# Groups of four, later sums and half-size GpSimd subtractions around the norms of a two-layer diffusion backbone step

## The chip, the cores and the metric

The kernel runs on one core of a Trainium2 chip, in one launch. The metric is the device time in microseconds; executions of one kernel are compared by their median.

## The reference, cut to what matters

The kernel computes one inference step for 512 latent and 128 context tokens of width 1024, in float32. Layer 0 has a Conformer convolution and a bidirectional retention behind one input projection; layer 1 has grouped-query attention with per-head RMS norms and rotary positions. Each layer ends in an MLP of width 4096, and a norm stands before every projection:

```python
for layer in range(DEPTH):
    sh1, sc1, g1, sh2, sc2, g2 = ...
    h = rmsnorm(x, norm_g[layer, 0]) * (1 + sc1) + sh1
    y = even_mixer(h, ...) if layer % 2 == 0 else blocked_attention(*gqa_project(h, ...)) @ odd_w_o[li]
    x = x + g1 * y
    h = rmsnorm(x, norm_g[layer, 1]) * (1 + sc2) + sh2
    x = x + g2 * (jnp.square(jax.nn.relu(h @ mlp_w1[layer])) @ mlp_w2[layer])
return rmsnorm(x, final_g), new_ret, new_k, new_v
```

## The kernel before

**Layout and precision.** The trunk x lies transposed in SBUF as xT, 8 chunks of 128 features by 640 tokens, and is worked on in two halves of 320 tokens. Each product keeps float32 accuracy by splitting both factors into a high and a low part (hH, hL; wH, wL) and adding three matmuls for each chunk k: high by high, high by low, low by high (product, L471). A group is one PSUM bank's result: 8 chunks, 24 matmuls. acc_full counts finished groups.

**Weights.** 96 tiles of 1024 x 256 pass through two slots (t % 2). For each, SyncE loads two halves into raw (load_tile, L350), ScalarE copies a half to wH (split, L977), and GpSimd subtracts to make wL (lo, L1361, L1366), one instruction of 1024 columns for each half, counted by wl_done. A split may begin only when the groups that read its slot are done; on ScalarE it stands in a fixed place among the evictions, with an acc_full value to wait for.

**A norm.** There are four with a projection behind them: norm 0 (the gate's projection), 1 (MLP of layer 0), 2 (QKV), 3 (MLP of layer 1). While the tile before still runs, VectorE adds its products to xT (residual, L1382), ScalarE squares xT (square, L985), VectorE adds the squares to ssum (add_squares, L1392), TensorE multiplies ssum by ones (stat, L598), ScalarE takes the root (std, L994), VectorE the reciprocal (L1409). Then for each half and chunk: VectorE makes vb (h_value, L1419), ScalarE hH (hi, L999), VectorE hL (h_lo, L1429), which counts h_ready. VectorE's order, with the residuals and squares of the second half put between the chunks of the first, is written out by hand in h_both (L1442), called from pair_ends (L1695) and for norm 1 at L1715. ScalarE's is in before_pair_ends (L1008), for norm 1 at L1163, and behind the norm in mlp_layer (L1223), the gate's lines (L1044) and the QKV loop (L1281).

**Behind a norm** TensorE does two weight tiles as a pair, so that the first half of h is used four times before the second is needed: tile_pair (L520) has groups 0 to 3 on half 0 (tile 0, tile 0, tile 1, tile 1) and 4 to 7 on half 1, two groups interleaved by k. stat(norm, 1) for the second half stands inside the first two groups, ahead of k = 4. The first half of the groups waits for banks by dve_free, the second by act_free. Slot 0 is released with group 5 and slot 1 with group 7: split(t0 + 2, 0, g0 + 6) and split(t0 + 3, 1, g0 + 8). In the MLP, ScalarE evicts a group with a relu to fr (L1219, two buffers), VectorE squares it to fs (L1735), ScalarE copies to fH (L1213), VectorE subtracts to fL (L1728). For the gate the eviction is a sigmoid (gate_out, L1049).

**QKV** (qkv_pair, L559) has the tokens in rows and 256 columns: ten groups, (tile, token block), in the order of QKV_PAIR, of which tile 0 makes the keys. Four more tiles follow (tile_n, L545; L897). VectorE norms and rotates each result (rope, L1782; its root is rope_std on ScalarE, L1255), TensorE turns it (turn_keys, L871, inside the first of the four tiles; turn_queries, L883, behind each), and ScalarE copies it out (turned_out, L1259, counted by tr_out, for which the next turn waits).

**Retention and convolution** (L1530 to L1624) run beside twelve weight tiles; VectorE does the convolution's 31 taps (L1543) there, 124 instructions of 655 columns.

## Time and profile before

| | |
|---|---|
| time of three runs | 1694.05 us median (1691.47 to 1695.34) |
| the profiled execution: its own time | 1695.47 us |
| its span | 1693.7 us |
| granted TensorE clock, mean over the span | 0.98 |
| TensorE busy | 1619.5 us (96%) |
| VectorE, ScalarE, GpSimd busy | 770.2, 528.1, 503.2 us |
| share of TensorE in the chain that ended last | 86% |

A row of a timeline gives start and duration in microseconds, engine, line, operation, output and inputs; equal neighbours are merged (x2), and the brackets give the idle time before it and what ended it. PE is TensorE, DVE VectorE, ACT ScalarE, POOL GpSimd. PEclk is the granted clock of TensorE as a share of its full 2.4 GHz.

### The profile page before, as it was taken

To read this page: it belongs to the slowest core of one execution; us is meant where nothing else is said; L and a number is where in the kernel's file an instruction comes from. 1 tells how busy PE (TensorE), PEld (TensorE's weight loads), DVE (VectorE), ACT (ScalarE), POOL (GpSimd) and SP (SyncE) were. 2 spreads that over 40 slices of the span, in tenths; PEclk is the share of its full clock that TensorE was granted. 3 is DMA by queue.
4 is the path that set the end of the run, shared out by engine and by line. 5 is a ranking of instruction groups with operands and counts; after the bars stand their busy time and mean duration, and the time that the engine had idled before them with its cause. 6 is when DMAs were issued, how large, how long until landed. Compare 5 with 4: busy or idle time off the path is not lost.

```text
span 1693.7 us, 27621 instructions
## 1 busy us (share of the span) xinstructions
PE 1619.5 (96%) x11934; PEld 1539.0 (91%) x11934; DVE 770.2 (45%) x1438; ACT 528.1 (31%) x986; POOL 503.2 (30%) x198
## 2 busy tenths in 40 slices
PE   5899998989899999999999989999999999999998
PEld 3899998979899999999999889556999999999997
DVE  4547675656662232242232865653572241331333
ACT  3413332324442132131232423543352131231332
POOL 0335234313233333333323233000233333333331
PEclk8999999999999999999999999999999999999999
DMA  8444333202243233343343122000222222222221
GB/s 298 141 158 127 117 113 125 88 26 69 87 149 125 94 132 125 125 148 105 105 142 111 57 75 69 13 1 1 79 85 75 75 76 75 75 75 75 75 75 63
DMA packets 131019, 162.16 MB, mean 96 GB/s; under 512 B 4433, under 2 KB 103633, under 8 KB 130897
## 3 DMA queue, kind: packets, MB, share of 16 engines
q1 hardware_dynamic: 129664, 159.34, 29.0%
q8 instruction: 94, 1.54, 0.4%
q10 hardware_dynamic: 1232, 1.05, 0.2%
q14 instruction: 29, 0.23, 0.0%
HBM read 156.44 MB, written 3.93 MB: 95 GB/s over the span
## 4 chain that ended last, share of the span: by engine, by line
PE 86%; DVE 8%; ACT 2%; POOL 1%; DMA 1%; issue 1%; SPq 0%; DVEq 0%; ACTq 0%
PE ps L479 74%; PE ps L590 2%; PE ps L944 2%; DVE hL L1429 2%; POOL wL L1366 1%; PE ps L909 1%; DMA pre_over_h<-in_ada_w 1%; PE ps L685 1%; DVE amx L1819 1%; PE ps L718 1%; DVE vb L1419 1%; ACT wH L983 1%; PE ps L610 1%; PE ps L923 1%; DVE xT L1387 1%
## 5 line engine op out<-in xcount | busy, mean ns | idle before, releaser
L1366 POOL TENSOR_TENSOR wL<-raw,wH 128x1024 fp32r<-128x1024 f32 x192 | 500.2, 2626 | 1158.1 <-ACT wH L983 1157.9
L479 PE MATMUL ps<-hH,wH 128*128 128x320 f32 x1536 | 482.6, 314 | 12.5 <-DVE hL L1429 7.1
L479 PE MATMUL ps<-hL,wH 128*128 128x320 f32 x1536 | 477.3, 311 | 0.0
L479 PE MATMUL ps<-hH,wL 128*128 128x320 f32 x1536 | 477.3, 311 | 0.0
L479 PE MATMUL ps<-fH,wH 128*128 128x320 f32 x1024 | 317.6, 310 | 0.0
L479 PE MATMUL ps<-fH,wL 128*128 128x320 f32 x1024 | 316.2, 309 | 0.0
L479 PE MATMUL ps<-fL,wH 128*128 128x320 f32 x1024 | 316.2, 309 | 0.0
L479 PEld LDWEIGHTS ps<-hH,wH 128*128 128x128 f32 x1536 | 291.2, 190 | 19.4 <-issue 9.5
L983 ACT ACTIVATE wH<-raw 128x1024 fp32r<-128x1024 f32 x192 | 193.0, 1051 | 346.9 <-PE ps L479 328.9
L479 PEld LDWEIGHTS ps<-hL,wH 128*128 128x128 f32 x1536 | 291.1, 190 | 0.6 <-issue 0.4
L479 PEld LDWEIGHTS ps<-hH,wL 128*128 128x128 f32 x1536 | 290.8, 189 | 0.0
L1387 DVE SCALAR_TENSOR_TENSOR xT<-ps,modT,xT 128x320 f32<-128x320 f32 (+2 forms) x264 | 107.4, 436 | 388.3 <-PE ps L479 388.2
L1735 DVE TENSOR_TENSOR fs<-fr 128x320 f32<-128x320 f32 x128 | 79.4, 621 | 265.0 <-ACT fr L1219 264.1
L479 PEld LDWEIGHTS ps<-fH,wH 128*128 128x128 f32 x1024 | 192.5, 188 | 1.7 <-issue 1.6
L479 PEld LDWEIGHTS ps<-fL,wH 128*128 128x128 f32 x1024 | 192.5, 188 | 0.1
L479 PEld LDWEIGHTS ps<-fH,wL 128*128 128x128 f32 x1024 | 192.5, 188 | 0.0
L479 PE MATMUL ps<-wH,hH 128*128 128x256 f32 x560 | 164.6, 294 | 4.8 <-POOL wL L1366 4.3
L479 PE MATMUL ps<-wL,hH 128*128 128x256 f32 x560 | 160.2, 286 | 0.0
L479 PE MATMUL ps<-wH,hL 128*128 128x256 f32 x560 | 160.2, 286 | 0.0
L1219 ACT ACTIVATE fr<-ps 128x320 f32<-128x320 f32 x128 | 55.7, 437 | 279.3 <-PE ps L479 279.2
L479 PEld LDWEIGHTS ps<-wH,hH 128*128 128x128 f32 x560 | 109.4, 195 | 6.4 <-issue 4.0
L479 PEld LDWEIGHTS ps<-wL,hH 128*128 128x128 f32 x560 | 109.4, 195 | 0.5 <-issue 0.2
(190 smaller groups left out, 1591.5 us busy)
## 6 DMA issues: line engine op xcount, KB each, us to landing
raw<-in_mlp_w SPq DMA_DIRECT2D x128, 512.0 KB, 3.9
ada<-in_ada_w SPq DMA_DIRECT2D x40, 1024.0 KB, 5.2
raw<-in_even_w_in SPq DMA_DIRECT2D x32, 512.0 KB, 5.8
raw<-in_even_w_out SPq DMA_DIRECT2D x12, 512.0 KB, 3.6
raw<-in_odd_w_qkv SPq DMA_DIRECT2D x12, 512.0 KB, 3.6
pre_over_h<-in_ada_w SPq DMA_DIRECT2D x2, 2048.0 KB, 14.9
pre_arena<-in_ada_w SPq DMA_DIRECT2D x2, 2048.0 KB, 18.7
raw<-in_odd_w_o SPq DMA_DIRECT2D x8, 512.0 KB, 3.4
```

The costliest lines, as they stand in the source:

```text
L479: last = nc.tensor.matmul(ps[:, bank, 0:width], a_, b_, start=(k == 0 and p_ == 0), stop=(k == nk - 1 and p_ == 2))
L590: last = nc.tensor.matmul(ps[32 * j:32 * j + 32, B_ADA, 0:P], siluc[:, 4 * part + k, :], by_lane[:, j], start=(part == 0 and k == 0), stop ...
L610: return nc.tensor.transpose(ps[:, bank, at:at + np_], src[p0:p0 + np_, tile, col0:col0 + P], ident[p0:p0 + np_, p0:p0 + np_])
L685: return nc.tensor.matmul(ps[:, bank, at:at + RV], kd_nat[:, r, tile, :], v_nat[:, tile, :], start=True, stop=True)
L718: last = nc.tensor.matmul(out, qdec[:, r, cs], S[:, r, n, :], start=False, stop=(r == 1))
L944: last = nc.tensor.matmul(ps[:, 6, :], va[:, vt, kv * P:(kv + 1) * P], pT[:, h % 2, n, :], start=(n == 0), stop=(n == 4))
L983: nc.scalar.activation(wH[:, slot, j * 1024:(j + 1) * 1024], raw[:, j, :], ACT.Copy).then_inc(wh_done, 1)
L1219: nc.scalar.activation(fr[:, n % 2, :], ps[:, n % 4, 0:HALF], ACT.Relu).then_inc(act_free, 1)
L1366: nc.gpsimd.tensor_tensor(wL[:, slot, cs], raw[:, j, :], wH[:, slot, cs].bitcast(F32), ALU.subtract).then_inc(wl_done, 1)
L1387: last = nc.vector.scalar_tensor_tensor(out=x, in0=ps[:, n % 4, c0 - half * HALF:c0 - half * HALF + w_], scalar=modT[:, gate_at + k, which ...
L1429: last = nc.vector.scalar_tensor_tensor(out=hL[:, k, c0:c0 + w_], in0=vb[:, k % 4, a_:a_ + w_], scalar=modT[:, SHIFT_AT[norm] + k, which:w ...
L1735: nc.vector.tensor_tensor(fs[:, n % 2, :], fr[:, n % 2, :], fr[:, n % 2, :], ALU.mult).then_inc(fs_done, 1)
```

## The change

- In all four pairs, the groups of the second half (4 to 7) are interleaved by k as one group of four, waiting for each bank at k = 0 (product's free). QKV_PAIR is reordered so that its groups 4 to 7 are token blocks 2 and 3 of both tiles, and 8 and 9 block 4.
- stat(norm, 1) stands ahead of k = 6 instead of k = 4, for norms 1, 2 and 3.
- ScalarE evicts groups 2 and 3 between the chunks of hH of the second half, fr has four buffers, and the splits of the next two tiles stand behind group 7's eviction (behind groups 8 and 9 for QKV).
- The orders of squares, hH chunks and splits before norms 1 to 3, and VectorE's order of residuals, squares and chunks, are changed.
- GpSimd subtracts in two pieces of 512 for each half tile.
- The first rotation waits for group 8 (act_free + 9) instead of 6, the keys are turned behind tile T_QKV + 2, and turn_queries(0) stands behind group 1 of the tile after, with turned_out(0) behind that group's eviction.

```diff
--- before.py
+++ after.py
@@ -104,7 +104,7 @@
 NAT_BANKS = (0, 1, 2, 3, 7)
-QKV_PAIR = ((0, 0), (0, 1), (1, 0), (1, 1), (0, 2), (0, 3), (0, 4), (1, 2), (1, 3), (1, 4))
+QKV_PAIR = ((0, 0), (0, 1), (1, 0), (1, 1), (0, 2), (0, 3), (1, 2), (1, 3), (0, 4), (1, 4))
@@ -249,7 +249,7 @@
         fL = place("fL", [P, KC, T], F32R)
-        fr = place("fr", [P, 2, HALF])
+        fr = place("fr", [P, 4, HALF])
@@ -468,12 +468,14 @@
         def _(pe):
-            def product(groups, nk, waits, width):
+            def product(groups, nk, waits, width, free=None):
...
                     waits(k)
-                    for bank, lhs, rhs in groups:
+                    for n, (bank, lhs, rhs) in enumerate(groups):
+                        if free and k == 0:
+                            free[n]()
@@ -517,7 +519,7 @@
-            def tile_pair(t, xH, xL, free, x_wait=None, hooks=None, nk=KC, nm=2, inside=None, together=1):
+            def tile_pair(t, xH, xL, free, x_wait=None, hooks=None, nk=KC, nm=2, inside=None, joint=None):
@@ -526,9 +528,11 @@
-                for n in range(0, 4 * nm, together):
-                    for q in range(n, n + together):
-                        free(q)
+                for ns in joint or [(n,) for n in range(4 * nm)]:
+                    n = ns[0]
+                    if len(ns) < 4:
+                        for q in ns:
+                            free(q)
@@ -537,8 +541,8 @@
                             x_wait(n // (2 * nm), n // nm % 2, k)
-                    product([group(q) for q in range(n, n + together)], nk, waits, HALF)
-                    for q in range(n, n + together):
+                    product([group(q) for q in ns], nk, waits, HALF, [lambda q=q: free(q) for q in ns] if len(ns) == 4 else None)
+                    for q in ns:
@@ -565,9 +569,10 @@
-                for ns in ((0, 1), (2, 3), (4, 5), (6,), (7, 8), (9,)):
-                    for q in ns:
-                        free(q)
+                for ns in ((0, 1), (2, 3), (4, 5, 6, 7), (8, 9)):
+                    if len(ns) < 4:
+                        for q in ns:
+                            free(q)
@@ -576,7 +581,7 @@
                             x_wait(n // 4, k)
-                    product([group(q) for q in ns], KC, waits, 256)
+                    product([group(q) for q in ns], KC, waits, 256, [lambda q=q: free(q) for q in ns] if len(ns) == 4 else None)
@@ -661,7 +666,7 @@
                       lambda half, tile, k: pe.wait_ge(h_ready, 8 * half + k + 1),
-                      {1: [lambda: strips(0)], 5: [lambda: strips(1)]}, together=2)
+                      {1: [lambda: strips(0)], 3: [lambda: strips(1)]}, joint=((0, 1), (2, 3), (4, 5, 6, 7)))
@@ -852,7 +857,7 @@
                           {1: [lambda: strips(M_MLP)], 3: [lambda: strips(M_MLP + 1)]} if layer == 0 else None,
-                          inside=(0, 4, lambda: stat(norm, 1, SUMS)), together=2)
+                          inside=(0, 6, lambda: stat(norm, 1, SUMS)), joint=((0, 1), (2, 3), (4, 5, 6, 7)))
@@ -893,11 +898,14 @@
                      pe.wait_ge(act_free, A_QKV + n - 4) if n > 4 else None,
-                     lambda half, k: pe.wait_ge(h_ready, 16 * 2 + 8 * half + k + 1), (0, 4, lambda: stat(2, 1, SUMS)))
+                     lambda half, k: pe.wait_ge(h_ready, 16 * 2 + 8 * half + k + 1), (0, 6, lambda: stat(2, 1, SUMS)))
...
                 tile_n(T_QKV + t, t % 2, lambda n, t=t: pe.wait_ge(act_free, A_QKV + 5 * (t - 1) + n + 1), NAT_BANKS,
-                       {1: [turn_keys]} if t == 2 else None)
-                turn_queries(t - 2)
+                       {1: [lambda: turn_queries(0)]} if t == 3 else None)
+                if t == 2:
+                    turn_keys()
+                else:
+                    turn_queries(t - 2)
@@ -1008,15 +1016,18 @@
                 std(norm, 0)
-                hi(norm, 0, range(0, 3))
                 square(norm, 12, v0, "tile")
+                hi(norm, 0, (0,))
                 square(norm, 13, v0, "tile")
+                hi(norm, 0, (1,))
                 split(t, 0, start - 2)
-                hi(norm, 0, range(3, 6))
+                hi(norm, 0, (2, 3))
                 square(norm, 14, v0, "tile")
+                hi(norm, 0, (4,))
+                split(t + 1, 1, start)
+                hi(norm, 0, (5,))
                 square(norm, 15, v0, "tile")
-                split(t + 1, 1, start)
-                hi(norm, 0, range(6, 8))
+                hi(norm, 0, (6, 7))
@@ -1044,7 +1055,6 @@
             hi(0, 0, range(6, 8))
-            hi(0, 1, range(0, 4))
@@ -1054,13 +1064,14 @@
             gate_out(1)
-            hi(0, 1, range(4, 8))
-            for n in range(2, 6):
+            hi(0, 1, range(0, 3))
+            gate_out(2)
+            gate_out(3)
+            hi(0, 1, range(3, 8))
+            for n in range(4, 8):
                 gate_out(n)
-            split(2, 0, G_GATE + 6)
-            gate_out(6)
-            gate_out(7)
-            split(3, 1, G_GATE + 8)
+            split(2, 0)
+            split(3, 1)
@@ -1165,18 +1176,20 @@
             square(1, 9, V_WC, "half")
-            hi(1, 0, range(0, 2))
+            hi(1, 0, (0, 1))
             square(1, 10, V_WC, "half")
-            hi(1, 0, range(2, 4))
             square(1, 11, V_WC, "half")
+            hi(1, 0, (2,))
             split(T_MLP0, 0, G_WC + 12)
+            hi(1, 0, (3,))
             square(1, 12, V_WC, "half")
-            hi(1, 0, range(4, 6))
+            hi(1, 0, (4,))
             square(1, 13, V_WC, "half")
+            split(T_MLP0 + 1, 1, G_MLP0)
+            hi(1, 0, (5,))
...
             square(1, 15, V_WC, "half")
-            split(T_MLP0 + 1, 1, G_MLP0)
-            hi(1, 0, range(6, 8))
+            hi(1, 0, (6, 7))
@@ -1214,23 +1227,24 @@
                     act.wait_ge(acc_full, g0 + 32 * g + n + 1)
-                    if n >= 2:
-                        act.wait_ge(fs_done, f0 + 16 * g + n - 1)
-                    nc.scalar.activation(fr[:, n % 2, :], ps[:, n % 4, 0:HALF], ACT.Relu).then_inc(act_free, 1)
-                    if n > 1 or g and n:
+                    if n >= 4:
+                        act.wait_ge(fs_done, f0 + 16 * g + n - 3)
+                    nc.scalar.activation(fr[:, n % 4, :], ps[:, n % 4, 0:HALF], ACT.Relu).then_inc(act_free, 1)
+                    if n and (g or n > 3):
...
-                hi(norm, 1, range(0, 4))
...
                 relu(0, 1)
-                hi(norm, 1, range(4, 8))
-                hidden_hi(0, 0)
-                for n in range(2, 6):
+                hi(norm, 1, range(0, 3))
+                relu(0, 2)
+                relu(0, 3)
+                hi(norm, 1, range(3, 8))
+                for n in range(3):
+                    hidden_hi(0, n)
+                for n in range(4, 8):
                     relu(0, n)
-                split(t0 + 2, 0, g0 + 6)
-                relu(0, 6)
-                relu(0, 7)
-                split(t0 + 3, 1, g0 + 8)
+                split(t0 + 2, 0)
+                split(t0 + 3, 1)
@@ -1278,24 +1292,25 @@
-            hi(2, 1, range(0, 2))
...
                 qkv_out(n, *QKV_PAIR[n], NAT_BANKS[QKV_BANK[n]])
-                if n == 0:
-                    hi(2, 1, range(2, 4))
                 if n == 1:
-                    hi(2, 1, range(4, 8))
-                if n == 6:
-                    split(T_QKV + 2, 0, G_QKV + 7)
+                    hi(2, 1, range(0, 2))
+                if n == 3:
+                    hi(2, 1, range(2, 8))
+                if n == 8:
+                    split(T_QKV + 2, 0, G_QKV + 9)
+            split(T_QKV + 3, 1, G_QKV + 10)
             rope_std(0)
-            split(T_QKV + 3, 1, G_QKV + 10)
...
                         rope_std(t - 1)
-                    if n == (3 if t == 2 else 1):
-                        turned_out(t - 2)
+                    if n == 1 and t > 2:
+                        turned_out(t - 3 if t == 3 else t - 2)
+                    if n == 3 and t == 3:
+                        turned_out(1)
@@ -1362,9 +1377,11 @@
                     pool.wait_ge(wh_done, 2 * t + j + 1)
-                    cs = slice(j * 1024, (j + 1) * 1024)
-                    nc.gpsimd.tensor_tensor(wL[:, slot, cs], raw[:, j, :], wH[:, slot, cs].bitcast(F32),
-                                            ALU.subtract).then_inc(wl_done, 1)
+                    for c0 in (0, 512):
+                        cs = slice(j * 1024 + c0, j * 1024 + c0 + 512)
+                        last = nc.gpsimd.tensor_tensor(wL[:, slot, cs], raw[:, j, c0:c0 + 512], wH[:, slot, cs].bitcast(F32),
+                                                       ALU.subtract)
+                    last.then_inc(wl_done, 1)
@@ -1441,6 +1458,8 @@
+                for step in later.get("first", ()):
+                    step()
@@ -1702,8 +1721,8 @@
-                h_both(norm, {0: [lambda: update(first + 4)], 2: [lambda: update(first + 5)], 3: [squares(2)],
-                              5: [lambda: update(first + 6)], 6: [lambda: update(first + 7)], 7: [squares(3)]})
+                h_both(norm, {0: [lambda: update(first + 4)], 1: [lambda: update(first + 5)], 3: [squares(2)],
+                              4: [lambda: update(first + 6)], 6: [lambda: update(first + 7)], 7: [squares(3)]})
@@ -1712,10 +1731,12 @@
                     add_squares(1, n // 2, "half")
-            h_both(1, {0: [lambda: wc(8)], 1: [lambda: wc(9), lambda: add_squares(1, 4, "half")],
-                       3: [lambda: wc(10)], 4: [lambda: wc(11), lambda: add_squares(1, 5, "half")],
-                       5: [lambda: wc(12)], 6: [lambda: wc(13), lambda: add_squares(1, 6, "half"), lambda: wc(14)],
-                       7: [lambda: wc(15), lambda: add_squares(1, 7, "half")]})
+            def wc_squares(q):
+                return lambda: add_squares(1, q, "half")
+
+            h_both(1, {"first": [lambda: wc(8)], 0: [lambda: wc(9), lambda: wc(10)], 1: [lambda: wc(11)],
+                       2: [wc_squares(4), lambda: wc(12)], 3: [lambda: wc(13), wc_squares(5)], 4: [lambda: wc(14)],
+                       5: [lambda: wc(15)], 6: [wc_squares(6)], 7: [wc_squares(7)]})
@@ -1732,7 +1753,7 @@
                             dve.wait_ge(f_ready, f0 + 16 * g + n - 1)
-                        nc.vector.tensor_tensor(fs[:, n % 2, :], fr[:, n % 2, :], fr[:, n % 2, :], ALU.mult).then_inc(fs_done, 1)
+                        nc.vector.tensor_tensor(fs[:, n % 2, :], fr[:, n % 4, :], fr[:, n % 4, :], ALU.mult).then_inc(fs_done, 1)
@@ -1784,7 +1805,7 @@
                 tab = tabs[:, 1 if r == 0 else 0]
-                dve.wait_ge(act_free, A_QKV + (5 * r + 5 if r else 7))
+                dve.wait_ge(act_free, A_QKV + (5 * r + 5 if r else 9))
...

```

## Rows read from the trace of the kernel before

**Rows 1.** The page, part 1: busy time, share of span, instructions of each engine.
```profile
PE 1619.5 (96%) x11934; PEld 1539.0 (91%) x11934; DVE 770.2 (45%) x1438; ACT 528.1 (31%) x986; POOL 503.2 (30%) x198
```

**Rows 2.** The list of waits: engine, line, releaser: us in total, times, longest.
```profile
PE ps L601 <- DVE ssum L1405: 9.9, 3, 4.0
...
PE ps L479 <- DVE hL L1429: 7.6, 6, 4.1
...
PE ps L479 <- DVE xT L1387: 5.4, 1, 5.4
...
PE ps L877 <- DVE kro L1808: 5.5, 1, 5.5
...
PE ps L479 <- POOL wL L1366: 4.3, 2, 3.6
...
PE ps L913 <- ACT qTa L1270: 2.5, 1, 2.5
```

**Rows 3.** Windows: length, busy us (count) of PE, PEld, DVE, ACT, POOL, PEclk, DMA.
```profile
1223.60:1236.20 12.60, 9.41 (x51) 8.39 (x50) 11.96 (x16) 5.32 (x9) 7.29 (x3) 0.86 0.43 129
...
944.70:957.40 12.70, 9.32 (x53) 8.44 (x52) 12.08 (x16) 5.29 (x9) 7.27 (x3) 0.73 0.48 147
...
460.10:471.70 11.60, 10.30 (x54) 9.69 (x58) 9.68 (x14) 4.57 (x8) 4.99 (x2) 0.79 0.16 46
...
263.70:270.50 6.80, 6.11 (x51) 5.24 (x50) 0.00 (x0) 2.39 (x3) 4.27 (x3) 0.50 0.50 150
...
992.30:997.50 5.20, 5.19 (x25) 5.20 (x26) 4.73 (x5) 0.30 (x1) 0.00 (x0) 0.50 0.02 3
```

**Rows 4.** TensorE timeline, last norm, two starts 24 matmuls apart: start, us, instruction.
```profile
1248.11 0.31 PE L479 MATMUL ps<-hH,wH 128*128 128x320 f32 x1
...
1251.63 0.31 PE L479 MATMUL ps<-hH,wH 128*128 128x320 f32 x1
```

**Rows 5.** VectorE timeline, last norm; and the group of full-width hL (busy, mean ns).
```profile
1228.54 0.54 DVE L1429 SCALAR_TENSOR_TENSOR hL<-vb,modT,hH 128x320 fp32r<-128x320 f32 x1
...
1231.08 4.12 DVE L1429 SCALAR_TENSOR_TENSOR hL<-vb,modT,hH 128x320 fp32r<-128x320 f32 x2 [0.61 <-ACT hH L1004]
...
L1429 DVE SCALAR_TENSOR_TENSOR hL<-vb,modT,hH 128x320 fp32r<-128x320 f32 x32 | 39.3, 1238 | 4.8 <-ACT hH L1004 4.8
```

**Rows 6.** GpSimd timeline, a plain tile and one beside the taps; its 128x512 group.
```profile
1253.01 4.79 POOL L1366 TENSOR_TENSOR wL<-raw,wH 128x1024 fp32r<-128x1024 f32 x2 [18.16 <-ACT wH L983]
...
244.82 19.68 POOL L1366 TENSOR_TENSOR wL<-raw,wH 128x1024 fp32r<-128x1024 f32 x2 [8.76 <-ACT wH L983]
...
L1374 POOL TENSOR_TENSOR y_nat<-y_nat,gfin 128x512 f32<-128x512 f32 x2 | 2.7, 1392 | 16.6 <-ACT y_nat L1196 16.6
```

**Rows 7.** VectorE timeline, norm 1: the residual update that releases TensorE.
```profile
459.34 0.66 DVE L1387 SCALAR_TENSOR_TENSOR xT<-ps,modT,xT 128x192 f32<-128x192 f32 x2
```

**Rows 8.** ScalarE timeline, last norm, behind groups 4 and 5.
```profile
1250.51 0.47 ACT L1213 ACTIVATE fH<-fs 128x320 fp32r<-128x320 f32 x1
...
1250.88 0.42 ACT L1219 ACTIVATE fr<-ps 128x320 f32<-128x320 f32 x1
...
1251.88 2.00 ACT L983 ACTIVATE wH<-raw 128x1024 fp32r<-128x1024 f32 x2
```

**Rows 9.** ScalarE timeline, gate norm, behind group 5.
```profile
73.16 0.88 ACT L1052 ACTIVATE sgate<-ps 128x320 f32<-128x320 f32 x2 [2.62 <-PE ps L479]
```

**Rows 10.** VectorE and ScalarE timelines, keys' and queries' rotation.
```profile
972.97 1.49 DVE L1788 TENSOR_TENSOR rn<-k_nat 128x1280 f32<-128x1280 f32 x1 [1.23 <-ACT k_nat L1279]
...
983.50 2.91 DVE L1804 TENSOR_TENSOR kro<-rn,tabs 128x640 f32<-128x640 f32 x1
...
989.23 0.81 DVE L1804 TENSOR_TENSOR kro<-rn,tabs 128x640 f32<-128x640 f32 x1
...
1002.03 0.39 ACT L1279 ACTIVATE q_nat<-ps 128x256 f32<-128x256 f32 x1 [2.49 <-PE ps L479]
...
1002.31 1.08 ACT L1264 ACTIVATE kTa<-ps 128x512 f32<-128x512 f32 x2
```

## The prediction

> **What bounds the kernel now.** I read the page first: TensorE is busy 96% of the span [rows 1], so time comes only from its idle time and its half-rate stretches. The list of waits then names what it waits for [rows 2]: the lower half of h, the keys' rotation, the residual, ssum, weight tiles and qTa. Around the norms that the change touches lie most of these (the last one, for qTa, and the weight tile do not). The windows show their size. From the end of the tile before to the end of the first two groups, the last norm takes 12.6 us and the QKV norm 12.7 [rows 3]. A group is 24 matmuls; 24 starts lie 3.52 us apart [rows 4], 0.147 each, and at 256 columns instead of 320 I take 0.8 of that, 0.12. So 48 matmuls need 7.0 and 5.8 us, and 5.6 and 6.9 us are lost. At norm 1 the loss is the 5.4 us wait [rows 2] and 11.6 - 7.0 = 4.6 us more [rows 3]. Behind the 3.6 us wait for a weight tile the granted clock stood at 0.50, which is 1.2 GHz, for 6.8 us, and behind the one for kro for 5.2 us of running matmuls [rows 3]. Half rate costs half of that, 3.4 and 2.6 us; I take 2.7, since a fall that begins within the wait leaves less behind it.
>
> The VectorE timeline shows why h is late [rows 5]. An undisturbed hL takes 0.54 us; the two at 1231.08 take 4.12 together; TensorE's last k of the first groups needs the second of them. The mean over the 32 full-width ones is 1238 ns, so (1.24 - 0.54) x 32 / 4 = 5.6 us per norm are spent blocked. GpSimd's subtractions lie exactly there [rows 6].
>
> **Parts that gain.** (a) *Pieces of 512.* One subtraction of 1024 takes 2.40 us. A piece costs between half of that (1.20) and the 1392 ns of the one 128x512 GpSimd group [rows 6]; I take 1.25, since the shorter of that group's two is 1.29. A blocked hL then waits for 1.25 at most. Per norm I expect some four blocks of 0.5 to 0.6 left of the 6.6 us in norms 2 and 3: a gain of 4.4 us each (bounds 0 and 6.6). The Trainium skill ("SBUF — State Buffer", "Who interferes with whom") says that a VectorE instruction with two SBUF inputs and a GpSimd one that reads SBUF exclude each other for the whole instruction. By that rule the shorter piece caps each block; the trace agrees (0.54 against 2.06 us for hL).
>
> (b) *Sums later, VectorE order.* stat(norm, 1) moves from k = 4 to k = 6. Part of the 9.9 us that TensorE waits for ssum [rows 2] goes, but the k's behind it need hL anyway, and the last hL comes later than the last sum. Alone it is worth the clock fall at most; I count it within the 4.4. At norm 1 the update that TensorE waited for ended at 460.0 [rows 7], 5.4 us after the tile's end. It moves ahead by some 8 us; then the weight is the bound (two copies and 2.5 us of GpSimd behind square 11), near the tile's end, and after that hL, which I carry forward as 4.8 us earlier (bounds 0 and the whole 10.0).
>
> (c) Gate norm: the last hL of the first half is blocked likewise; one piece less gives 1.1.
>
> (d) *Keys later.* The 5.5 us wait for kro [rows 2] and the 2.6 of clock behind it [rows 3] go: 8.1.
>
> Gains: 1.1 + 4.8 + 4.4 + 4.4 + 8.1 = 22.8 us.
>
> **Parts that cost.** (e) *Groups of four.* Groups 4 to 7 use both weight slots until their last k. Before, slot 0 was free after group 5, two groups (7.0 us) before the pair's end, and its split ran beside groups 6 and 7. Now split(2, 0) and split(t0+2, 0) stand behind the last eviction, and TensorE has nothing else to do but wait for wL. From the start that TensorE's next matmul could have (0): the first eviction can begin at -1.1 (three times 3 matmuls earlier, less 0.2 to notice). At the MLP norms ScalarE does four relus at 0.43 and four fH copies at 0.47 [rows 8], which ends at 2.5, then half a split, 1.0, then two pieces, 2.5, and 0.2 of semaphores: 6.2. After 12 matmuls (8.0) the second half of the weights (8.7) holds it 0.7 more: 6.9 us each. At the gate it is four sigmoids at 0.44 [rows 9] in place of eight instructions: 0.7 + 1.0 + 2.5 + 0.2 = 4.4, and 0.7: 5.1. At QKV the pair (8, 9) ends the stage, and the split is behind group 8: 4.4 again for the first half; the second stands against rope(0)'s VectorE work, where VectorE's and GpSimd's instructions take turns (a product of 0.81 took 2.91 [rows 10]), so 2.1 more: 6.5. The quads' own gain, more time for each k of the second half, is at most a few tenths: the six waits for hL [rows 2] lie ahead of first halves or within them, but for one.
>
> (f) *Clock behind these.* The same kind of stall, 3.6 us for a weight tile [rows 2], was followed by 6.8 us at 0.50 [rows 3]. Four stalls at 2.7: 10.8 us (bounds 0 and 3.4 each).
>
> (g) *Queries.* turn_queries(0) now stands after group 1 of the next tile and needs turned_out(0), which ScalarE does only behind that group's eviction and behind rope_std(2). At least 0.39 for that eviction and 0.54 x 3 for the copies [rows 10], with 0.7 for the root and the semaphores 2.7 us, pass with TensorE idle. But rope_std(2) waits for VectorE's third rope, and the first one now starts some 8.6 us (three groups) later relative to TensorE, since the k_nat copies end with group 8. A rope is 1.49 x 3 + 0.81 x 6, about 10 us with its waits, more while pieces alternate with it (the 2.91 again). Carried forward, the wait is up to 9.6. I take 7.0, nearer the upper end because POOL is busy beside the first rope for six pieces, and 2.7 for the clock: 9.7.
>
> (h) In the convolution (130 to 340 us) a piece more has to get its turn: one stall of 3.6 us becomes 0.5 longer.
>
> Costs: 5.1 + 6.9 + 6.9 + 6.5 + 10.8 + 9.7 + 0.5 = 46.4. Net +23.6 us. The profiled execution took 1695.5 (span 1693.7 and 1.8 around it), so 1719.1; it lies 1.4 above the median of the runs shown, so 1717.7 against that median. Called 1718. What lies beside other work costs nothing: fr's two more buffers, SP's loads (raw is filled one tile ahead), and the doubled count of GpSimd instructions (0.1 more for two pieces, on an engine busy 30% [rows 1]).
>
> **Rivals.** *A milder loss:* the clock stays up behind most new stalls and turn_queries(0) waits for ScalarE alone. Then 23.6 - 10.8 - 2.7 - 4.3 = +6 with all clock falls gone, +9 with one left: about 1703. For it: the wait for turned_out alone is as short as the 2.5 us for qTa [rows 2]. Against: the weight stall of 3.6 us had its fall, and the new ones are longer.
>
> *Starved pieces:* GpSimd's two subtractions at 244.8 took 19.7 us together [rows 6], because VectorE's taps followed one another without a break. Where the first of two pieces gets in and the second does not, a weight tile comes late by a run of taps, up to the 15 us that were waited there (19.7 less 2 x 2.4). I put it at 9: 1727. Against: a piece gets in whenever VectorE waits for TensorE, as it does in this stage once for each head. The skill's rule in the same section, that whichever issues first gets the ports, knows no starvation and would leave this out; the 19.7 us speak against it here.
>
> *The other side, faster:* all loss before the first two groups' ends goes (5.6 + 6.9 + 10.0 + 1.1 + 8.1 = 31.7) and the clock stays up behind the new stalls, which are then 5.1 + 6.9 + 6.9 + 4.4 + 2.7 = 26.0: 5.7 us faster, 1688. The place is the wait for wL after each group of four; it decides when the sum of those stalls falls below the gain. Against: the first k's of a norm need hL within a microsecond of the reciprocal, and VectorE has 12 us of work [rows 3] in a stretch where TensorE needs 7.
>
> *The sums and pieces do not do what they say* (PE stays bound by the same last hL): gains 9.2 instead of 22.8, 1731.
>
> **Numbers.** Likeliest +24 (0.68; its own range 1706 to 1730), milder 0.12, starved 0.07, no gain at the norms 0.06, faster 0.07. The likeliest gives the time, 1718. Adding the milder case below and the two above gives 1700 to 1734; what lies outside, the faster case and the tails, is under 0.2. A measurement of this kernel tells a change of over 0.2% (3.4 us) from none. Faster by that 0.05; within it 0.04; slower 0.91.
>
> **What would show it.** After each norm's last group of four, a wait of TensorE for wL, 4 to 7 us, where rows 2 have 4.3 in all; half-rate stretches behind them; GpSimd 128x512 x384 with a mean near 1.3; the mean of hL from 1238 to below 900 ns; the wait for kro gone and one for kTa or qro at turn_queries(0). Wrong if TensorE goes on without a gap after those groups, or if that wait is under 3 us.

## The result, and the profile after

| | before | after |
|---|---|---|
| median of 4 runs, us | 1694.69 (1691.47 to 1695.43) | 1734.03 (1732.38 to 1736.44) |
| profiled execution's span, us | 1693.7 | 1734.6 |
| mean granted clock | 0.980 | 0.968 |

The ratio is 1.0235, 95% interval 1.0221 to 1.025: the change makes the kernel 39 us slower, where 24 were forecast. The time lies just above the upper end of the forecast's range, 1734.

First the page of the changed kernel, part 1, against [rows 1]:

```profile
PE 1630.6 (94%) x11934; PEld 1547.5 (89%) x11934; DVE 736.4 (42%) x1438; ACT 529.4 (31%) x986; POOL 544.4 (31%) x390
```

TensorE has the same 11934 matmuls and 94% of a longer span: idle time and half-rate time came on top. VectorE's busy time fell by 34 us: its instructions stand behind shorter GpSimd pieces, and the kernel before with these pieces alone, further below, has 731.4 us. Nothing came of it. The group of full-width hL has a mean of 793 ns where [rows 5] has 1238, and 15.2 us of idle time ahead where 4.8 stood:

```profile
L1446 DVE SCALAR_TENSOR_TENSOR hL<-vb,modT,hH 128x320 fp32r<-128x320 f32 x32 | 25.3, 793 | 15.2 <-ACT hH L1012 15.2
```

The list of TensorE's waits (columns as in [rows 2]) shows what was added:

```profile
PE ps L481 <- POOL wL L1382: 24.8, 6, 5.8
PE ps L481 <- DVE hL L1446: 19.3, 5, 5.3
PE ps L894 <- ACT kTa L1281: 11.1, 1, 11.1
...
PE ps L606 <- DVE ssum L1422: 4.3, 2, 3.9
PE ps L595 <- DMA ada<-in_ada_w: 4.2, 2, 3.6
```

Three are the forecast ones: wL from 4.3 to 24.8 us, kTa in place of kro, and ssum from 9.9 down to 4.3. Two are not: hL went up from 7.6 to 19.3 us, and the waits for a transfer of ada from 1.2 to 4.2 us. Where the time went can be read more closely by setting the n-th matmul of one trace against the n-th of the other. The lag is how much later a matmul starts in the changed kernel. It stands still between the stages, and each stage below is taken from one such level to the next:

| stage | forecast, us | grown lag, us |
|---|---|---|
| gate (norm 0 to its third tile) | +6.7 | +10.6 |
| norm 1 | -4.8 | -1.5 |
| behind MLP 0's group of four | +9.6 | +7.8 |
| norm 2 | -4.4 | +1.1 |
| behind QKV's group of four | +9.2 | +5.6 |
| keys | -8.1 | -8.0 |
| first queries | +9.7 | +12.5 |
| norm 3 | -4.4 | +3.4 |
| behind MLP 1's group of four | +9.6 | +7.6 |
| convolution | +0.5 | -1.6 |

The second column adds up to 37.5; 3.5 more lie scattered, 2.3 of them ahead of the gate, and the last matmul is 41.0 us late. Of the gate's 10.6, its norm is -1.0 and the rest +11.5. The three norms behind it brought a loss of 3.0 us where a gain of 13.6 was forecast. That difference of 16.6 us is as large as the whole error, 39 less 24.

Behind a group of four the forecast chain is there. At MLP 0 the last matmul starts at 505.06, ScalarE's split stands behind the last eviction, then come two pieces of GpSimd, then TensorE:

```profile
505.06 0.31 PE L481 MATMUL ps<-hH,wL 128*128 128x320 f32 x1
...
507.46 1.99 ACT L991 ACTIVATE wH<-raw 128x1024 fp32r<-128x1024 f32 x2
...
508.58 4.95 POOL L1382 TENSOR_TENSOR wL<-raw,wH 128x512 fp32r<-128x512 f32 x4 [31.61 <-ACT wH L991]
...
511.21 0.61 PE L481 MATMUL ps<-hH,wH 128*128 128x320 f32 x1 [5.83 <-POOL wL L1382]
511.61 0.47 PE L481 MATMUL ps<-hL,wH 128*128 128x320 f32 x1
511.88 0.47 PE L481 MATMUL ps<-hH,wL 128*128 128x320 f32 x1
```

What TensorE waits for at norm 3 is a lower half of h, behind the split that the change moved. ScalarE's timeline there (start, us, instruction, idle before and releaser):

```profile
1253.68 0.56 ACT L1012 ACTIVATE hH<-vb,modT 128x320 fp32r<-128x320 f32 x1
1256.15 1.06 ACT L991 ACTIVATE wH<-raw 128x1024 fp32r<-128x1024 f32 x1 [1.91 <-DMA raw<-in_mlp_w]
1260.58 1.06 ACT L991 ACTIVATE wH<-raw 128x1024 fp32r<-128x1024 f32 x1 [3.37 <-DMA raw<-in_mlp_w]
1261.55 0.55 ACT L1012 ACTIVATE hH<-vb,modT 128x320 fp32r<-128x320 f32 x1
```

and GpSimd's, VectorE's and TensorE's, a few rows each:

```profile
1249.42 5.85 POOL L1382 TENSOR_TENSOR wL<-raw,wH 128x512 fp32r<-128x512 f32 x4 [17.14 <-ACT wH L991]
1257.29 2.50 POOL L1382 TENSOR_TENSOR wL<-raw,wH 128x512 fp32r<-128x512 f32 x2 [2.02 <-ACT wH L991]
...
1262.12 1.21 DVE L1446 SCALAR_TENSOR_TENSOR hL<-vb,modT,hH 128x320 fp32r<-128x320 f32 x1 [5.46 <-ACT hH L1012]
...
1257.76 0.31 PE L481 MATMUL ps<-hH,wL 128*128 128x320 f32 x1
1263.39 0.64 PE L481 MATMUL ps<-hH,wH 128*128 128x320 f32 x1 [5.32 <-DVE hL L1446]
```

The split of the second tile now stands ahead of hi for k = 5. Its first cast waits 1.91 us and its second 3.37 us for raw to be filled: GpSimd had been reading raw for the tile before until 1255.27. ScalarE works in order, so hH for k = 5 comes at 1261.55, VectorE has been idle for 5.46 us, and TensorE for 5.32. Of all casts of MLP weights, the list of ScalarE's waits says, for before and for after (10.1 us of the latter at norms 1 and 3, and 13.9 behind the two groups of four):

```profile
ACT wH L983 <- DMA raw<-in_mlp_w: 3.5, 3, 1.5
```

```profile
ACT wH L991 <- DMA raw<-in_mlp_w: 24.0, 8, 5.5
```

At the gate, SP's own timeline shows the second thing that was missed, with TensorE's rows beside it:

```profile
87.86 2.84 SPq L356 DMA_DIRECT2D raw<-in_even_w_in  x2
90.75 8.47 SPq L368 DMA_DIRECT2D ada<-in_ada_w  x2
...
87.98 0.38 PE L481 MATMUL ps<-hH,wH 128*128 128x320 f32 x1 [4.13 <-POOL wL L1382]
...
96.86 1.94 PE L595 MATMUL ps<-ada,siluc 128*32 128x128 f32 x32 [3.59 <-DMA ada<-in_ada_w]
```

The fourth weight tile's load may be issued only when GpSimd has done with the third's raw, which the group of four made late; the ada load is the next thing in the same queue. So one late tile gives two waits. (The kernel before waits 1.2 us for the same transfer.) Windows (columns as in [rows 3]) at norm 1, behind MLP 0's group of four, at norm 3 and at the gate's second wait:

```profile
474.10:480.90 6.80, 4.97 (x15) 4.13 (x16) 5.63 (x7) 2.75 (x7) 2.75 (x2) 0.50 0.00 1
511.20:515.00 3.80, 3.79 (x14) 3.80 (x15) 0.00 (x0) 0.20 (x1) 2.33 (x2) 0.50 0.51 148
1262.50:1269.30 6.80, 5.87 (x19) 5.03 (x20) 6.15 (x7) 1.53 (x4) 1.97 (x2) 0.50 0.33 103
95.20:102.00 6.80, 5.14 (x44) 4.67 (x45) 0.00 (x0) 0.04 (x1) 2.56 (x3) 0.50 0.40 129
```

Each of these waits has a stretch at 1.2 GHz around it; the forecast expected such stretches only behind the groups of four and the queries.

### The profile page after: what moved, and what is told of

It is laid out like the page before. It is cut to its first block, busy times and chain, and to the rows that moved or that the text cites. A ratio compares the mean times of both kernels' runs of the same rounds, so it can differ in the third digit from the quotient of the medians.

```text
span 1734.6 us, 27787 instructions
## 1 busy us (share of the span) xinstructions
PE 1630.6 (94%) x11934; PEld 1547.5 (89%) x11934; DVE 736.4 (42%) x1438; ACT 529.4 (31%) x986; POOL 544.4 (31%) x390
## 4 chain that ended last, share of the span: by engine, by line
PE 85%; DVE 5%; POOL 3%; DMA 3%; ACT 2%; issue 1%; SPq 0%; DVEq 0%; ACTq 0%
PE ps L481 74%; POOL wL L1382 3%; PE ps L595 2%; PE ps L952 2%; PE ps L917 1%; DMA pre_over_h<-in_ada_w 1%; PE ps L690 1%; DVE amx L1840 1%; DMA ada<-in_ada_w 1%; PE ps L723 1%; ACT wH L991 1%; PE ps L615 1%; PE ps L931 1%; PE ps L651 1%; DMA raw<-in_mlp_w 1%
## 5 line engine op out<-in xcount | busy, mean ns | idle before, releaser
L1382 POOL TENSOR_TENSOR wL<-raw,wH 128x512 fp32r<-128x512 f32 x384 | 541.5, 1442 | 1158.1 <-ACT wH L991 1157.9
L1756 DVE TENSOR_TENSOR fs<-fr 128x320 f32<-128x320 f32 x128 | 74.2, 581 | 300.0 <-ACT fr L1232 298.9
L481 PEld LDWEIGHTS ps<-wH,hH 128*128 128x128 f32 x560 | 109.4, 195 | 14.6 <-issue 8.4
```

The source lines that it names most:

```text
L481: last = nc.tensor.matmul(ps[:, bank, 0:width], a_, b_, start=(k == 0 and p_ == 0), stop=(k == nk - 1 and p_ == 2))
L1382: last = nc.gpsimd.tensor_tensor(wL[:, slot, cs], raw[:, j, c0:c0 + 512], wH[:, slot, cs].bitcast(F32), ALU.subtract)
L1756: nc.vector.tensor_tensor(fs[:, n % 2, :], fr[:, n % 4, :], fr[:, n % 4, :], ALU.mult).then_inc(fs_done, 1)
```

## The experiments

Every kernel was timed against the kernel before on its chip, and a ratio to before is given with its 95% interval. A gain over the changed kernel is the difference of the two ratios times 1694 us (the changed kernel's is 1.0235); with both intervals it is good to some 4 us.

### The groups of four

Pairs everywhere, then at the gate alone, then at the two MLPs alone. In the changed kernel:

```diff
-joint=((0, 1), (2, 3), (4, 5, 6, 7)))
+joint=((0, 1), (2, 3), (4, 5), (6, 7)))
-                for n in range(4, 8):
-                    relu(0, n)
-                split(t0 + 2, 0)
-                split(t0 + 3, 1)
+                for n in range(2, 6):
+                    relu(0, n)
+                split(t0 + 2, 0, g0 + 6)
+                relu(0, 6)
+                relu(0, 7)
+                split(t0 + 3, 1, g0 + 8)
```

and likewise the evictions of the gate and QKV, with the order of hi halves around them. For QKV the first rope's root and the group for which the first rotation waits go back as well, so this run undoes a little more than the groups.

> The changed kernel with its second halves in pairs again: gate, both MLPs and QKV take (4, 5), (6, 7) where it has (4, 5, 6, 7), and the order of evictions, hi halves and splits around them goes back with it. The sums asked for later, the pieces of 512, the split ahead of hi 5 and the keys turned one tile later stay. Theory (the groups of four cost the waits for the weights of tile t+2 behind them, 4.1, 5.8, 4.3 and 5.8 us with their spells of half clock, the wait for ada at the gate's third tile, and the late third rope): gate 11 us, MLPs 6 and 7, QKV 5, queries 9 back, so 30 to 38 us faster than the changed kernel, 1696 to 1704 us. Rival (the waits for weights come from the pieces and GpSimd's later start, not from the groups): the waits for wL stay over 4 us each and the gain stays under 15 us, 1719 us or more. Rival two: pairs bring back the waits of the kernel before at the halves (7.6 us for hL in all) and the gain is 20 to 25 us.

Measured: 1699.92 us, 1.0039 (1.0024 to 1.0054), 33 us faster than the changed kernel, the size that the theory gave. The waits for wL fell from 24.8 us to this, with the convolution's old one in it:

```profile
PE ps L481 <- POOL wL L1382: 5.0, 3, 3.8
```

The wait at the first queries stayed, 8.5 us instead of 11.1, so most of it is not the groups' doing and that part of the theory fell; nor did the waits for hL go: 17.5 us.

> The changed kernel with its gate alone in pairs (4, 5), (6, 7) again, with the order of evictions, hi halves and splits of the kernel before there; MLPs and QKV keep their groups of four. Theory (by the two traces compared matmul by matmul the gate loses 11.8 us: 4.1 us for wL of the third tile, 3.7 for ada, the rest the two spells of half clock around them): 10 to 13 us faster than the changed kernel, 1721 to 1724 us, no wait for ada. Rival (the ada load ahead of the fourth weight tile gave 9.2 us by itself, so the group of four costs only what is left of it beside that load, or the two overlap less): 15 us or more faster, under 1719 us. Rival two (the gate's loss is only its two waits, 7.8 us): 7 to 9 us, 1725 to 1727 us.

Measured: 1724.10 us, 1.0168 (1.0145 to 1.0192): 11.3 us, the theory's, and the 11.5 of the lags. The wait for wL is gone, and the one for ada is 1.5 us, near the 1.2 of the kernel before, though SP's order is the changed kernel's.

> The changed kernel with the two MLPs alone in pairs again (evictions, hi halves and splits with them); gate and QKV keep their groups of four. Theory (the waits for wL of 5.8 us behind each group, with the half clock at both, 6.1 and 7.1 us by matmul): 11 to 15 us faster than the changed kernel, 1719 to 1723 us. Rival (the prediction's term, 6.9 us of wait and 2.7 us of clock each): 18 to 20 us, 1714 to 1716 us. Rival two (undone here, the wait for weights returns one tile on, since GpSimd is behind anyway): under 7 us, 1727 us or more.

Measured: 1718.40 us, 1.0137 (1.0116 to 1.0157): 16.6 us, between the theory (11 to 15) and the forecast's own term (18 to 20), and within 4 us of both. The lags give 7.8 + 7.6 = 15.4. What is left of the 33 us for QKV and the queries is 33.2 - 11.3 - 16.6 = 5.3, a rough figure since it is made of three such differences; QKV's group alone was not undone in any run.

### The place of the split at the norms

One place back, behind square 15. In the changed kernel, and likewise at norm 1:

```diff
                 hi(norm, 0, (4,))
-                split(t + 1, 1, start)
                 hi(norm, 0, (5,))
                 square(norm, 15, v0, "tile")
+                split(t + 1, 1, start)
                 hi(norm, 0, (6, 7))
```

> The changed kernel with one thing undone: at norms 1 to 3 the cast-and-copy pair of the second weight tile (split of tile t+1) stands behind square 15 again, not ahead of the fifth hi half. Theory (ScalarE, which works in order, stands ahead of hi 5 waiting for raw's transfer, 3.0 and 1.8 us at norm 1, 1.9 and 3.4 us at norm 3, so hH and hL of k = 5 come late): TensorE's waits for hL of 4.66, 4.77 and 5.32 us at the three norms fall to under 1.5 us each, the 0.5 clock behind them at two of the three goes: 10 to 13 us faster than the changed kernel, some 1721 to 1724 us. Rival (VectorE's own chain of halves sets the waits, and the split's place is nothing to it): the three waits stay over 4 us, the time within 2 us of 1734. Second rival: the split put back delays the weights of tile t+1 and the wait turns up at the next tile's first weights, the sum within 4 us of 1734.

Measured: 1730.13 us, 1.0215 (1.0195 to 1.0235): 3.4 us, no more. The theory asked for 10 to 13, so as it stood it fell. The waits for hL shrank only to 3.2, 3.4 and 2.6 us, and they had moved from k = 5 to k = 6. ScalarE's timeline at norm 1 shows what still stands ahead of hi 6:

```profile
469.60 1.04 ACT L991 ACTIVATE wH<-raw 128x1024 fp32r<-128x1024 f32 x1
471.75 1.06 ACT L991 ACTIVATE wH<-raw 128x1024 fp32r<-128x1024 f32 x1 [1.11 <-DMA raw<-in_mlp_w]
472.71 1.00 ACT L1012 ACTIVATE hH<-vb,modT 128x320 fp32r<-128x320 f32 x2
```

Two casts and one transfer, 3.1 us from the first cast's start to that of hi 6. So the next kernel puts the split behind hi 6 and 7 as well:

```diff
                 square(norm, 15, v0, "tile")
-                split(t + 1, 1, start)
                 hi(norm, 0, (6, 7))
+                split(t + 1, 1, start)
```

> The changed kernel with the split of the second weight tile at norms 1 to 3 behind all hi halves of the first half (k = 6 and 7 too); one place earlier, behind square 15, its two casts still stood ahead of hi 6 and one of them waited 1.1 us for raw's transfer, so that TensorE's wait only moved from k = 5 to k = 6 (3.2, 3.4 and 2.6 us) and 3.9 us came back. Theory (ScalarE in order behind a cast that needs raw is the whole of these waits): the three waits fall to under 1.2 us each, 8 to 12 us faster than the changed kernel, 1722 to 1726 us. Rival (VectorE's chain of mean square, root and products has its own end there once TensorE comes earlier): the waits stay at 2 to 3 us, the time is that of the place behind square 15, 1729 to 1731 us. Second rival: weights of tile t+1 come late instead and a wait for wL or wH appears within the next tile.

Measured: 1716.29 us, 1.0133 (1.0116 to 1.0149): 17.3 us, more than the 8 to 12 expected, and as much, within the error, as the 16.6 that the norms were off. TensorE's waits in the window of norm 3, where 5.3 us for hL stood:

```profile
PE ps L481 <- POOL wL L1381: 1.7, 1, 1.7
```

The three waits for hL, 14.6 us in sum, are gone. For wL there are 1.9 us in the window of norm 1, where the changed kernel had 1.0, and 2.0 and 1.7 us at norms 2 and 3, so the second rival is true too, but small. That leaves 14.6 - 0.9 - 2.0 - 1.7 = 10.0 us of waits less. The rest is the clock: the changed kernel has 6.8 us at 1.2 GHz beginning at 474.1, 969.0 and 1262.5; this one has nothing near the first and the third, and 3.4 us at the second. At half rate those 17.0 us less are up to 8.5 us. By the lags between these two traces some 15 us of the gain arise at the three norms.

### SP's queue at the gate, and the first queries

The third ada load issued ahead of the fourth weight tile's:

```diff
+                if t == 2:
+                    load_ada(t)
                 if t < 3:
                     load_tile(t + 1, k8(even_w_in[0], (CONV + 256, 0, 256)[t]))
-                load_ada(t)
+                if t != 2:
+                    load_ada(t)
```

> The changed kernel with one order changed on SP's queue: at the gate the third ada transfer is issued ahead of the fourth weight tile's, whose issue waits until GpSimd has done with raw. Theory (TensorE's wait of 3.7 us for ada at 96.9 us is the queue standing behind that issue): the wait goes, 3.5 us and with the half clock before it up to 7 us are gained: 1727 to 1731 us. Rival (TensorE stands there for wL of the same tile anyway, which the ada wait hides): the wait changes its name to GpSimd's wL or stays by half, and the gain is under 1.5 us.

Measured: 1724.55 us, 1.0183 (1.0164 to 1.0203): 8.8 us, the theory's mechanism and by the ratio more than its size. From 80 to 100 us TensorE now has a single wait:

```profile
PE ps L484 <- POOL wL L1385: 4.1, 1, 4.1
```

The wait of 3.6 us is gone, and 6.8 us at 1.2 GHz stand there in place of 3.4 and 6.8: 3.6 + 1.7 = 5.3 us, and the lag between the two traces shrinks by 5.3 us there. It also shrinks at places that the edit does not touch, by 2.4 us ahead of the gate and by 2.5 near 1190 us, where a stretch at 1.2 GHz is missing. So 5.3 us is what the edit is shown to give; the other 3.5 are within what such a difference is good to. The gate alone in pairs gave 11.3 us, and it takes most of this wait away as well, so the two gains don't add up.

The first queries' copies ahead of the third rope's root:

```diff
+                    if n == 1 and t == 3:
+                        turned_out(0)
                     if n == 1:
                         rope_std(t - 1)
-                    if n == 1 and t > 2:
-                        turned_out(t - 3 if t == 3 else t - 2)
+                    if n == 1 and t > 3:
+                        turned_out(t - 2)
```

> The changed kernel with one order changed on ScalarE: the copies of the first turned queries (turned_out(0)) stand ahead of the root of the third rope, not behind it. Theory (TensorE's 11.2 us before it turns the first queries is ScalarE waiting 8.8 us for VectorE's third rope, ahead of copies whose source has long been ready): the wait falls to 5 to 7 us, the time by 4 to 6 us, to 1728 to 1730 us. Rival (the copies themselves wait for the second rope, which ends hardly earlier): the wait stays at 10 to 11 us and the time within 1.5 us of 1734. Second rival: the third rope's root comes later and its wait moves on to the turning of the next queries: sum unchanged, the wait found one tile later.

Measured: 1730.42 us, 1.0217 (1.0196 to 1.0238): 3.0 us by the ratio, 3.6 by the medians, a little under the theory and within its error. In the changed kernel ScalarE's timeline has the root first, behind 8.77 us of waiting, and then the copies:

```profile
1035.83 0.30 ACT L1271 ACTIVATE rss<-rss,eps 128x10 f32<-128x10 f32 x1 [8.77 <-DVE rss L1811]
1036.04 1.06 ACT L1278 ACTIVATE kTa<-ps 128x512 f32<-128x512 f32 x2
```

In the kernel of this run the list of waits has for the same place

```profile
PE ps L894 <- DVE qro L1831: 5.0, 1, 5.0
```

The wait fell from 11.1 to 5.0 us, and its releaser changed: below ScalarE's order lies VectorE's second rope. The lag between the two traces shrinks by 5.6 us there, inside the theory's 4 to 6.

### Parts of the change alone, on the kernel before

GpSimd's pieces alone:

```diff
-                    cs = slice(j * 1024, (j + 1) * 1024)
-                    nc.gpsimd.tensor_tensor(wL[:, slot, cs], raw[:, j, :], wH[:, slot, cs].bitcast(F32),
-                                            ALU.subtract).then_inc(wl_done, 1)
+                    for c0 in (0, 512):
+                        cs = slice(j * 1024 + c0, j * 1024 + c0 + 512)
+                        last = nc.gpsimd.tensor_tensor(wL[:, slot, cs], raw[:, j, c0:c0 + 512], wH[:, slot, cs].bitcast(F32),
+                                                       ALU.subtract)
+                    last.then_inc(wl_done, 1)
```

> The kernel before with GpSimd's subtractions in pieces of 512 and nothing else. Theory (a VectorE write of hL that shares the port with a GpSimd piece takes 1.1 to 1.2 us beside 512 elements and 2.3 us beside 1024, so the pieces shorten each wait for hL at the norms): the waits for hL, 7.6 us in all, fall by 2 to 4 us, the time by 2 to 5 us, to 1689 to 1692 us. Rival (twice as many GpSimd instructions starve or lag behind VectorE's back-to-back work and weights come late): waits for wL appear, 1697 us or more. Rival two (pieces do not matter in this order of work): within 1.5 us of 1694.

Measured: 1692.64 us, 0.9995 (0.9985 to 1.0004), the second rival. The instructions do become shorter; this is the group of full-width hL in this kernel, 927 ns against 1238 in [rows 5]:

```profile
L1431 DVE SCALAR_TENSOR_TENSOR hL<-vb,modT,hH 128x320 fp32r<-128x320 f32 x32 | 29.3, 927 | 10.7 <-ACT hH L1004 10.7
```

Beside it stands the idle time ahead of them, 10.7 us where [rows 5] has 4.8. VectorE finishes sooner and waits longer for ScalarE's hH. TensorE's waits for ssum fell from 9.9 to 5.4 us and those for hL rose from 7.6 to 11.3. The limit was one engine further up.

The sums later alone:

```diff
-inside=(0, 4, lambda: stat(norm, 1, SUMS))
+inside=(0, 6, lambda: stat(norm, 1, SUMS))
```

> The kernel before with the sums of the second half asked for ahead of k = 6, not of k = 4, at norms 1 to 3 and nothing else. Theory (TensorE now does the products of k = 4 and 5 in the time it stood for ssum, but then stands for hL of k = 6, which ScalarE and VectorE give at the same moment as before): the waits for ssum, 9.9 us, mostly go and waits for hL of 2 to 3 us each appear; net 0 to 4 us faster, 1690 to 1694 us. Rival (as forecast in the prediction: the whole 4.4 to 4.8 us per norm is gained): 1680 to 1683 us. Rival two (the mean comes later by the products that go ahead, so root and third product are late and the wait is larger behind): 1696 us or more.

Measured: 1698.08 us, 1.0024 (1.0013 to 1.0036): 4 us slower, the second rival. Waits for ssum of 3.0 us each at norms 2 and 3 became waits for hL; the window of norm 3 has 0.3 us for hL in the kernel before and here

```profile
PE ps L479 <- DVE hL L1429: 3.4, 4, 1.8
```

while the second half's mean, root and reciprocal all start later.

The keys later alone:

```diff
                 tile_n(T_QKV + t, t % 2, lambda n, t=t: pe.wait_ge(act_free, A_QKV + 5 * (t - 1) + n + 1), NAT_BANKS,
-                       {1: [turn_keys]} if t == 2 else None)
-                turn_queries(t - 2)
+                       {1: [lambda: turn_queries(0)]} if t == 3 else None)
+                if t == 2:
+                    turn_keys()
+                else:
+                    turn_queries(t - 2)
```

with the copies in the change's order.

> The kernel before with one part of the change alone: the keys turned a tile later and the first queries inside the fourth tile, with ScalarE's copies in the change's order (root of the third rope ahead of the first queries' copies). Theory (the keys' wait of 5.5 us and its half clock go, 8 us, and a wait of 8 to 9 us ahead of the first turned queries takes their place, as in the kernel with pairs: 8.8 us): net -1 to +3 us, 1693 to 1697 us. Rival (as the prediction had it, the cheap end: 2.7 us of wait only): 5 to 7 us faster, 1687 to 1689 us. Rival two: the queries' wait depends on the group of four in QKV and is under 2 us here: 1686 us or less.

Measured: 1698.72 us, 1.0033 (1.002 to 1.0046): 5.6 us slower (3.4 to 7.8), just outside the theory's -1 to +3. The wait is there without any group of four:

```profile
PE ps L889 <- ACT kTa L1270: 8.6, 1, 8.6
```

So 5.5 us for kro were traded for 8.6 us for kTa. By the lags 8.0 us are gained at the keys, as forecast, and 10.7 lost at the queries.

### Versions that beat both

Pairs, the split behind hi 7, the first queries' copies first; of the change stay the later sums, the pieces, the order of VectorE's and ScalarE's work within the norms and the later keys. No new edit: the diffs are above.

> Three of the mended parts together: second halves in pairs with their order of evictions, the split of the second tile behind hi 6 and 7 at norms 1 to 3, and the first turned queries' copies ahead of the third rope's root. What stays of the change: sums asked for at k = 6, pieces of 512, the keys turned one tile later. Pairs alone gave 1699.9. Theory (the three parts are separate waits and add up: norms 5.0, 4.8 and 4.0 us of waits for hL less some 1.5 each, queries 8.8 less 3 to 4): 11 to 15 us under 1699.9, so 1685 to 1689 us, and under the kernel before. Rival (with the waits gone the next one at the same place takes over, as it did when the split moved by one place): 1695 to 1699 us, no better than before.

Measured: 1680.16 us, 0.9918 (0.9904 to 0.9932). The parts add up: from 1.0235 take 0.0196, 0.0102 and 0.0018, which gives 0.9919. So the gains at the norms can be had, but not with the order that the change gave to ScalarE. By the lags between the kernel before and this one, norms 1 to 3 gain 7.2, 1.9 and 3.3 us, 12.4 in sum, where the prediction had 13.6.

The kernel before with only the later sums and the split behind hi 7:

> The kernel before with two things: the sums asked for ahead of k = 6 at norms 1 to 3 (alone: 1698.1) and the split of the second tile behind hi 6 and 7. VectorE's order, GpSimd's pieces of 1024 and everything else as before. Theory (the sums later pay only when ScalarE's hi 6 and 7 do not stand behind a cast that waits for raw): 5 to 9 us faster than before, 1685 to 1689 us. Rival (the change's VectorE order or its pieces are needed too, since VectorE writes hL beside a GpSimd piece of 1024 at 2.3 us): 1692 to 1697 us.

Measured: 1690.81 us, 0.9983 (0.9973 to 0.9994). Between the two theories: 3 us faster than before, and 7 faster than with the later sums alone. At norm 1 the old wait stands unchanged; this kernel has VectorE's old order, and it is the new one that moves the update ahead:

```profile
PE ps L479 <- DVE xT L1387: 5.4, 1, 5.4
```

In the fast kernel it is gone, and its window at norm 1 has 1.9 us for wL alone.

The fast kernel with GpSimd's subtractions whole again:

> The fast kernel of the last batch (pairs, split behind hi 7, first queries' copies first: 1680.2) with GpSimd's subtractions in pieces of 1024 again. Theory (pieces matter only where VectorE's hL is what TensorE waits for; here its waits are for wL, by 1 to 2 us at each norm, and the first 512 do not release anything earlier since the count goes up after the second): within 2 us of 1680.2. Rival (three products beside pieces of 1024 take 2.3 us instead of 1.2 us each, and hL is late again at each norm): 4 to 8 us slower, 1684 to 1688 us.

Measured: 1680.90 us, 0.9925 (0.991 to 0.9939), the same time as with pieces. The pieces are worth nothing here either.

The fast kernel with the keys back in the third tile, and the first root asked for ahead of the last three evictions:

```diff
                 if n == 6:
                     split(T_QKV + 2, 0, G_QKV + 7)
-            rope_std(0)
+                    rope_std(0)
```

> The fast kernel of the last batch (1680.2) with the keys turned where the kernel before turned them, inside the third tile, and the root of the first rope asked of ScalarE right behind the split after the seventh eviction, 5.4 us earlier, not behind the tenth. Theory (the keys' wait of 5.5 us ends with the first rope, and that starts when its root is there; the queries' wait of 3.7 us and its half clock go, since there is a tile more for the second rope): keys' wait under 2 us, no wait ahead of the first queries, 3 to 7 us faster, 1673 to 1677 us. Rival (VectorE's own work before the root, squares and sums of the rope, ends late too, so an earlier root changes nothing): keys' wait 4 to 6 us and its half clock back, 1680 to 1684 us.

Measured: 1674.27 us, 0.989 (0.9872 to 0.9907), 19 us faster than before, the best of all, and within the theory's 1673 to 1677. Its waits from 965 to 1010 us, where before had 5.5 us for kro and the fast kernel 3.7 for qro:

```profile
PE ps L894 <- DVE qro L1823: 0.5, 1, 0.5
PE ps L882 <- DVE kro L1823: 0.2, 1, 0.2
```

The two edits were made together, so no run says how much each of them gives.

## Why the prediction was wrong, point by point

- **Bound.** Right: TensorE, by its idle and half-rate time.
- **(a) and (b), the norms.** This step failed. It took 4.8 us of gain from VectorE's new order and twice 4.4 from shorter blocks, and asked only what VectorE and GpSimd do. Of the diff's ScalarE order it used the squares and the weight, not that split(t + 1, 1) had moved ahead of hi 5. The sentence that SP's loads cost nothing because raw is filled one tile ahead was the very error: raw holds one tile, each half is filled again only after GpSimd's subtraction, and a split right behind another must wait for a whole subtraction and a transfer. Measured: a loss of 3.0 us by the lags in place of 13.6 of gain, and 17.3 us back when the split was moved. What VectorE was to do, it did: the wait of 5.4 us for the update at norm 1 is gone, and 4.7 us for hL stood in its place. "The k's behind it need hL anyway" was right: the later sums alone brought no gain. The bound of 6.6 us for norms 2 and 3 comes from no row; the forecast's own losses there were 6.9 and 5.6.
- **(a), the pieces.** Shorter blocks as forecast, to 793 ns where under 900 was named, but without worth by two runs. At norm 3 an hL takes 1.21 us beside a piece and 0.55 alone, so the trace again agrees with the Trainium skill ("SBUF — State Buffer", "Who interferes with whom") that the two exclude each other; it is just not what TensorE waits for.
- **(c) Gate norm and the gate's group of four.** The norm's 1.1 us is there: a wait for hL of 1.43 us fell to 0.35. The wait for wL is there with 4.13 us where 4.4 + 0.7 was forecast. The wait for ada is the second failed step, again "SP's loads cost nothing": behind the norm 11.5 us by the lags (11.3 by the run) against 7.8.
- **(e), (f) Groups of four.** Mechanism right, size too high. The MLP waits are 5.8 us, not 6.9: the 0.7 for the second half of the weights never came, since TensorE reached it later, twelve starts 0.27 us apart at half rate, 3.2 us, where GpSimd needs 2.5. QKV's wait was 4.2, without the 2.1 for rope(0). With the clock 7.8 and 7.6 us by the lags, or 16.6 for both by the run, against 9.6 each. What the lags have beyond the waits, 2.0, 1.8 and 1.4 us at MLP 0, MLP 1 and QKV, is less than the 2.7 forecast for each: at MLP 0 only 3.8 of the 6.8 us at half rate lay behind the wait.
- **(d) Keys** 8.0 us against 8.1. **(g) Queries** 11.1 us of wait, above the upper bound of 9.6: the guess "nearer the upper end" was right in its direction and too low. By one run 3.0 us of the time, or 5.6 by the lags, hang on ScalarE's order; the wait below it, 5.0 us, is VectorE's.
- **(h) Starved pieces.** TensorE's wait in the convolution was 3.8 us against 3.6 of before; that the lag fell by 1.6 us there is the clock, 3.4 us at 1.2 GHz in place of 6.8. The four pieces at 257.69 took 19.95 us together, as long as the two whole ones of [rows 6]. The first took 16.13 of them, behind VectorE's taps, which end at 271.29, and the other three 3.9, so the rival did not occur. The rule of the Trainium skill ("SBUF — State Buffer", "Who interferes with whom") that issue order decides who blocks does not say what a piece meets that comes amid a run of taps; here it waited for the end of the run.
- **Rivals.** That nothing is gained at the norms had a chance of 0.06 and a time of 1731. It is what happened by the trace, for a reason that it did not name: VectorE was not the bound, ScalarE's order was. That its time is so near 1734 is in part luck, since other terms were off as well.

Errors of unlike sign hide in the sum. By the lags the norms and the gate cost 20.5 us more than forecast and the queries 2.8 more; the weights behind MLPs and QKV cost 7.4 less and the convolution 2.1 less.

## What to carry to other kernels

When a diff reorders an engine that works in order, list what each moved instruction waits for at its new place, transfers and single buffers included, and who is queued behind it; do the same for the queue that issues the loads. Interleaving more groups over k leaves more time for each k, but it holds every weight slot to the end, and where the next weights must still be cast and subtracted, TensorE waits for that whole chain. And before an instruction is made shorter to cure a wait, look at what it itself waits for: here VectorE had only been late with what ScalarE gave it.

## What was not expected of the hardware

Waits of 4.6 to 5.3 us at the norms cost nearly double: they fell by 10.0 us in sum and the time by 17.3, with 17.0 us fewer at 1.2 GHz. Two GpSimd subtractions of 512 columns take little more than one of 1024 (2.50 us for two at 1257.29 against 2.40 in the kernel before; over the whole kernel GpSimd's busy time rose from 503.2 to 544.4 us, 0.2 us for each pair), so splitting costs little, and it also brought nothing. Beside VectorE's back-to-back taps four pieces took 19.95 us, 16.13 of them the first; in the kernel before the first of two whole ones took 17.22. Less their own 1.3 and 2.4 us, both stood some 14.8 us: a shorter instruction got in no sooner.
